# Routed experts: the third pair's rows also picked in SBUF, the first reads of scattered rows one pair later

## The reference, cut to what matters

```
h = LayerNorm(ALPHA * h + mix)                    # 520 rows of 1024
h = LayerNorm(ALPHA * h + HierMoE(h))
# HierMoE: best of 4 groups, then the top 2 of its 8 experts
hid = silu(x @ w_gate[e]) * (x @ w_up[e])         # 1024 -> 256, 32 experts
y  += weight[row, e] * (hid @ w_down[e])          # 256 -> 1024
```

## Time and profile before

| what | us |
|---|---|
| median of three runs | 1031.05 |
| lowest, highest | 1030.75, 1032.7 |
| the profiled execution: device time | 1032.45 |
| the profiled execution: its span | 1030.6 |
| mixer, up to the first weights of the experts | about 656 |
| experts, 656 to the end of the last `down` | about 328 |
| gather of results and last LayerNorm | about 46 |

### The profile page before, as it was taken

One profiled execution on the slowest core, in us unless ns is written; L12 is line 12 of the kernel. 1 busy time (PEld: TensorE's weight loads), 2 busy tenths in 40 slices (PEclk: granted clock), 3 DMA queues, 4 the chain that ended last, 5 costly groups with the idle time before them and its releaser, 6 DMA issues.

```text
span 1030.6 us, 11835 instructions
## 1 busy us (share of the span) xinstructions
PE 838.6 (81%) x4513; PEld 578.1 (56%) x4513; DVE 469.7 (46%) x1025; ACT 265.1 (26%) x654; POOL 183.6 (18%) x146
## 2 busy tenths in 40 slices
PE   6999899999967788699999899878199978856910
PEld 5987789888846666478888444555133323321300
DVE  6996476575648665674344143350021101100158
ACT  4221444343452267354321011100011100000100
POOL 2663534341045540000000000020000000000030
PEclk9999899999979888899999899969599989978965
DMA  8322264451251123551622200599889999999452
GB/s 293 98 63 72 87 241 164 164 184 62 95 182 50 30 83 131 205 206 74 245 82 82 82 0 1 202 424 423 341 334 430 424 423 428 425 377 426 167 186 83
DMA packets 38809, 207.92 MB, mean 202 GB/s; under 512 B 9069, under 2 KB 9677, under 8 KB 28193
## 3 DMA queue, kind: packets, MB, share of 16 engines
q1 hardware_dynamic: 29056, 172.28, 42.9%
q0 software_dynamic: 5136, 18.36, 5.2%
q10 hardware_dynamic: 4560, 16.52, 4.0%
HBM read 169.00 MB, written 38.05 MB: 201 GB/s over the span
## 4 chain that ended last, share of the span: by engine, by line
PE 39%; issue 31%; DVE 19%; DMA 4%; POOL 2%; ACT 2%; SPq 1%; POOLq 0%; DVEq 0%; ACTq 0%
PE bank L561 7%; PE bank L568 7%; PE bank L570 6%; PE bank L569 6%; DVE r_f L1424 5%; DMA y_f<-scr_bc 2%; PE bank L722 2%; PE bank L754 1%; DVE y_f L1503 1%; DMA x_f<-in_conv_state 1%; PE bank L682 1%; DVE y_f L1572 1%; POOL scr_x L2085 1%; PE bank L753 1%; PE bank L758 1%
## 5 line engine op out<-in xcount | busy, mean ns | idle before, releaser
L568 PE MATMUL bank<-r_r,w_r 128*128 128x268 f32 x416 | 125.3, 301 | 10.8 <-DVE w_r L1401 10.2
L569 PE MATMUL bank<-y_r,w_r 128*128 128x268 f32 x416 | 121.6, 292 | 0.0
L570 PE MATMUL bank<-r_r,w_r 128*128 128x268 f32 x416 | 121.5, 292 | 0.0
L945 PE MATMUL bank<-x_f,r_f 128*64 128x512 f32 x256 | 87.6, 653 | 13.4 <-DMA x_f<-in_w_gu 10.8
L569 PE MATMUL bank<-w_r,r_r 128*128 128x512 f32 x240 | 96.6, 402 | 0.0
L568 PE MATMUL bank<-x_r,r_r 128*128 128x512 f32 x200 | 82.4, 412 | 16.0 <-DVE w_r L1704 12.0
L568 PEld LDWEIGHTS bank<-r_r,w_r 128*128 128x128 f32 x416 | 81.4, 196 | 15.9 <-DVE w_r L1401 10.2
L1900 DVE TENSOR_TENSOR y_f<-bank,y_f 128x256 f32<-128x256 f32 x17 | 7.2, 424 | 166.4 <-ACT y_f L1327 154.2
L569 PEld LDWEIGHTS bank<-y_r,w_r 128*128 128x128 f32 x416 | 81.3, 196 | 0.0
L570 PEld LDWEIGHTS bank<-r_r,w_r 128*128 128x128 f32 x416 | 81.1, 195 | 0.0
L570 PE MATMUL bank<-x_r,w_r 128*128 128x512 f32 x200 | 80.7, 404 | 0.0
(11 more groups left out here) (334 smaller groups left out, 1561.1 us busy)
## 6 DMA issues: line engine op xcount, KB each, us to landing
x_f<-in_w_gu SPq DMA_DIRECT2D x16, 2048.0 KB, 31.6
w_f<-in_w_gu SPq DMA_DIRECT2D x12, 2048.0 KB, 22.3
w_f<-in_w_f SPq DMA_DIRECT2D x26, 512.0 KB, 4.4
scr_x<-y_f SPq DMA_DIRECT2D x25, 512.0 KB, 6.1
w_f<-in_w_d SPq DMA_DIRECT2D x12, 1024.0 KB, 24.1
x_f<-in_w_d SPq DMA_DIRECT2D x11, 1024.0 KB, 29.5
w_f<-in_w_t SPq DMA_DIRECT2D x5, 2048.0 KB, 8.1
y_f<-in_w_gu SPq DMA_DIRECT2D x5, 2048.0 KB, 28.9
```

The source lines that it names most:

```text
L568: pe.matmul(out, ah, bh, start=start, stop=False)
L569: pe.matmul(out, ah, bl, start=False, stop=False)
L570: return pe.matmul(out, al, bh, start=False, stop=stop)
L945: ins = pe.matmul(out[half, :], XT[:, k, half], wgu[s][:, k, :], start=(k == 0), stop=(k == KC - 1))
```

## The change

`N_HOT` becomes 3, so pair 2 is picked out of `h1` as pairs 0 and 1 are. Its ten DVE instructions are not in `dve_route` but at the head of `dve_experts`, with matrices `hot_last[t]` in the place of buffer X[0]; `iota_hot` gets a third part; `near` moves to another address. ACT's wait on `sc_out` and its first two reads (now for pairs 3 and 4) come after pair 1, and the read for pair 4 is no longer issued inside pair 1. The scaling of `h1` by ALPHA on DVE (L1915, L1916) comes in pair 3 and no more in pair 2.

```diff
-N_HOT = 2
+N_HOT = 3
+N_HOT0 = 2
...
+        hot_last = [cut(R1 + P * t, P) for t in range(NT)]
+        iota_hot = cut(RX + N_HOT0 * P, N_HOT * P)
...
             def pick_x(b):
...
-                    pe.wait_ge(S["hot_dv"], t + 1)
+                    pe.wait_ge(S["hot_dv"], NT * (b // N_HOT0) + t + 1)
+                    chosen_rows = hot[t][0:r, P * b:P * (b + 1)] if b < N_HOT0 else hot_last[t][0:r, :]
...
                     act.wait_ge(S["xtr_mm"], b + 2)
-                    if b and b + 3 < FIRST or b == FIRST:
+                    if b > 1 and b + 3 < FIRST or b == FIRST:
                         load_x(act, b + 3 if b < FIRST else FIRST + 2)
...
-                if b == 0:
+                if b == 1:
                     act.wait_ge(S["sc_out"], 16 * 2 * NT)
                     load_x(act, N_HOT)
                     load_x(act, N_HOT + 1)
...
+            for t in range(NT):
+                dve_link[0](v.tensor_scalar(hot_last[t], iota_hot[:, N_HOT0 * P:], near[:, t:t + 1], None, ALU.is_equal))
+                v.scalar_tensor_tensor(hot_last[t], iota_hot[:, N_HOT0 * P:], near[:, NT + t:NT + t + 1], hot_last[t],
+                                       ALU.is_equal, ALU.add).then_inc(S["hot_dv"], 1)
             v.wait_ge(S["xtr_mm"], 1)
             v.wait_ge(S["rt_dv"], 4)
             empty_x("xt_ev")
```

More of the change, by code:

```diff
@@ L277, in build @@
         far, base = more(2 * NT), more(2 * NT)
-        near = more(2 * NT)
+        near = cut(RX + (N_HOT0 + N_HOT) * P, 2 * NT)
         thr8 = more(EPG)
@@ L290, in build @@
         wdn = [cut(b, DE // P, D) for _, b in slot_at]
-        hot = [*(cut(R1 + 2 * D + N_HOT * P * t, N_HOT * P) for t in range(NT - 1)), cut(RX, N_HOT * P)]
-        iota_hot = cut(RX + N_HOT * P, N_HOT * P)
+        hot = [*(cut(R1 + 2 * D + N_HOT0 * P * t, N_HOT0 * P) for t in range(NT - 1)), cut(RX, N_HOT0 * P)]
+        hot_last = [cut(R1 + P * t, P) for t in range(NT)]
+        iota_hot = cut(RX + N_HOT0 * P, N_HOT * P)
         X, XT = [cut(R1, D), cut(C1, D)], cut(R1 + D, KC, P)
@@ L927, in pick_x @@
                     r = tile_rows(t)
-                    pe.wait_ge(S["hot_dv"], t + 1)
+                    pe.wait_ge(S["hot_dv"], NT * (b // N_HOT0) + t + 1)
+                    chosen_rows = hot[t][0:r, P * b:P * (b + 1)] if b < N_HOT0 else hot_last[t][0:r, :]
                     for k in range(KC):
                         ins = pe.matmul(pb[k // 4][:, (k % 4) * P:(k % 4 + 1) * P], h1[0:r, t, k * P:(k + 1) * P],
-                                        hot[t][0:r, P * b:P * (b + 1)], start=(t == 0 and k % 4 == 0),
+                                        chosen_rows, start=(t == 0 and k % 4 == 0),
                                         stop=(t == NT - 1), skip_group_check=True)
@@ L1869, in dve_route @@
             for t in range(NT):
-                link(v.tensor_scalar(hot[t], iota_hot, near[:, t:t + 1], None, ALU.is_equal))
-                v.scalar_tensor_tensor(hot[t], iota_hot, near[:, NT + t:NT + t + 1], hot[t], ALU.is_equal, ALU.add)\
-                 .then_inc(S["hot_dv"], 1)
+                link(v.tensor_scalar(hot[t], iota_hot[:, 0:N_HOT0 * P], near[:, t:t + 1], None, ALU.is_equal))
+                v.scalar_tensor_tensor(hot[t], iota_hot[:, 0:N_HOT0 * P], near[:, NT + t:NT + t + 1], hot[t],
+                                       ALU.is_equal, ALU.add).then_inc(S["hot_dv"], 1)
             link(v.tensor_reduce(extra, over[:, :, :], AX, ALU.add))
```

## The result

The changed kernel takes 1019.46 us (median of four runs, 1016.01 to 1021.6) against 1031.01 for the kernel before on the same chip: ratio 0.9881, 95% interval 0.9849 to 0.9914, a gain of 11.6 us where 10.2 were forecast. Left out of all times are single executions that took hundreds of us longer than the others of their kernel (1449 us once in `hole_back`, 1691 and 4586 for the kernel before).

The account below looks back on a forecast made before the run. The prediction took the weights' stream to bound the experts' stage: closing its hole (8.5 to 9.6 us) and dropping pair 2's read (1.3) give 10.2, so 1032.45 becomes 1022.2 profiled, median 1020.8 us, range 1018.5 to 1025.5.

Parts of the forecast that it names:

- The bound: Experts' stage: the weights' stream limits it; PE's 22.4 us wait counts only through the hole it tears there.
- The 0.24 us of `iota_hot`: Routing chain: one more instruction for the third part delays pair 0 by 0.24 us, hidden by SP's full queue.
- the 6 us in hand: Pair 3's rows, expected at 744.2 us, could land as late as 750 without opening a hole in the stream.
- the first wait for weights: PE in the experts' stage: expected still around pair 8 or earlier, and longer than before.
- The hole: DMA between 740 and 755 us, share 0.44 and 151 GB/s: expected to close, worth 8.5 to 9.6 us.
- The sum: Experts' stage: closed hole plus pair 2's dropped read, together 9.7 to 10.8 us, taken as 10.2.
- the read's 1.2: Weights' stream: pair 2's read of 0.52 MB falls away, forecast as 1.3 us at 417 GB/s.
- the hole by share: DMA's dry stretch sized by engine share, 15 x (1 - 0.44 / 1.01) = 8.5 us.
- The late read: Rival: pair 3's rows land after 750 us, moving part of the hole; at 755, time 1025.8 us; chance 0.12.
- The port case: Rival: `hot_last` on DVE locks POOL's scatter issue, ending the scatter up to 4.0 us later; 1022.5 us; chance 0.05.
- The extra half block: Rival: weights issued behind it at 929.05 us do not move forward; gain 7.4 us, time 1023.6; chance 0.07.
- The prediction's one pairing: POOL's DMA issue at 690.60 us, 0.96 us long, with DVE's copy starting inside it: taken as no stretching.

Follow-up runs that it names:

- `hole_back`: Changed kernel with one more wait on SP: pair 4's down weights wait until pair 3's rows are turned; 1019.05 us, ratio 0.9891 to the kernel before.
- `hole_long`: Changed kernel with SP holding pair 4's down weights and all later loads until pair 4's rows are turned; 1034.35 us, ratio 1.005 to the kernel before.
- `less_bytes`: Changed kernel reading only the first half of the down weights of experts 14 to 17, all compute instructions kept; 1015.74 us.
- `pe_extra`: Changed kernel with the eight transposes for pair 5 made six times; 1019.25 us.
- `fourth_pick`: Changed kernel with pair 3's rows picked too, ten more DVE instructions, and the first reads of rows after pair 2; 1019.71 us.
- `before_again`: The kernel before the change, unchanged, run once more; 1028.41 us, ratio 0.9992.

## Why the prediction was right

**The bound.** Shown: a hole without the stall costs (`hole_long`); 5.0 us worth of bytes less save 4.0 to 5.8 us by the count and 3.5 by the median time (`less_bytes`); 4.4 us more of PE work cost nothing that can be told from none (`pe_extra`).

**The steps.** The 0.24 us of `iota_hot` are 0.20: three instructions now take 0.68 us against 0.48. `hot_last` takes five times 0.58 = 2.9 us, inside the 2.0 to 4.0, and DVE still waits 1.27 us before pair 0's copy:

```profile
668.41 0.68 DVE L1861 TENSOR_SCALAR x_f<-bank 128x128 f32<-128x128 f32 x3
...
680.56 0.28 DVE L1926 TENSOR_SCALAR r_f<-x_f 128x128 f32<-128x128 f32 x1
680.88 0.35 DVE L1927 SCALAR_TENSOR_TENSOR r_f<-x_f,r_f 128x128 f32<-128x128 f32 x1
681.14 0.28 DVE L1926 TENSOR_SCALAR r_f<-x_f 128x128 f32<-128x128 f32 x1
...
684.84 0.69 DVE L1900 COPY r_f<-bank 128x512 f32<-128x512 f32 x1 [1.27 <-PE bank L933]
```

The pick takes 9.2 us from its start to that of the hidden turn (713.22 to 722.45), as forecast. From pair 0's start, SP's loads for pairs 4 and 5 go out after 41.4 and 48.3 us, as forecast (41.4 and 48.3). The read of pair 3 went out 43.9 us behind pair 0's start against 42.7, took 11.2 us (729.54 to 740.73) against 10, and from the transposes to gate and up lie 8.25 us against 6.8: the granted clock had fallen to the lower level, 0.50, in the wait.

```profile
739.00:741.00 2.00, 0.27 (x2) 0.28 (x3) 0.00 (x0) 0.00 (x0) 0.00 (x0) 0.50 1.06 444
```

So pair 3 started 3.9 us later than forecast (63.4 against 59.4 from pair 0's start). This cost nothing, as the 6 us in hand said, and it is evidence of its own: from pair 0's start PE gained 6.9 us at pair 3, the stage 10.8 (339.1 to 328.3). One sign came otherwise: the first wait for weights is not at pair 8 or earlier but at pair 9 (5.29 us at 828.95), which fits: PE gained less than the stream and so caught up with it later.

**A term that may be too small.** The hole closed wholly. The sum, 10.2 (9.7 to 10.8), against 11.2 in the first pair of profiles; over both pairs the counts are 373.7 and 362.5 on average, again 11.2. By bytes the hole is 15 x (1 - 151 / 426) = 9.7 us, and the stretch behind it, 412 against 424 GB/s over 25 us, adds 0.7; with the read's 1.2 that is 11.6. By this reading I took a value too near to the hole by share and ended the hole at 755 us too early. It is not shown: the counts of one kernel differ by 1.8 us, the later runs on one chip have medians of 1029.06 and 1019.25, 9.8 us apart, and the read's 1.2 us never showed by itself (`fourth_pick`).

**The rivals.** The late read did not come: the rows landed 55.1 us behind pair 0's start, and the forecast had room until 58.4 (750). The port case did not come either: from POOL's first issue to the first read of rows pass 49.3 us in both profiles of the changed kernel and 48.7 and 49.3 in the two of the kernel before. POOL's ten issues take 12.4 us from first to last end, against 12.3 before, one at 1.05 us and the others at 0.89 to 0.98, and the slowest of the scatter's DMAs lands after 37.8 us and not 37.3:

```profile
681.49 0.98 POOL L2092 DMA_INDIRECT scr_x<-r_f,small_f  x1 [0.31 <-issue]
682.77 1.05 POOL L2092 DMA_INDIRECT scr_x<-r_f,small_f  x1 [0.30 <-issue]
```

The Trainium skill ("SBUF — State Buffer", section "SBUF: two separate sides") lets a VectorE instruction in a two-port mode hold up such issues. Here ten instructions from SBUF to SBUF beside three of them left no more than that 0.1 us, and no row shows whether they work in such a mode. The prediction's one pairing was not the only one in its trace: two short instructions from SBUF to SBUF (0.21 and 0.18 us, at 685.5) stand beside POOL's first issue there, which took 0.95 us. The extra half block moved with the stream: pair 13's wait is 7.02 us against 7.68, and from its gate and up to the end lie 86.3 us in both profiles.

## What to carry to other kernels

Where a stage is bound by a stream of loads, as this one is, a stall of the computing engine costs only the hole that it makes in the stream, by way of the loads that its late instructions release; size the gain by the DMA rows (missing bytes by the full rate) and not by the wait's length. Follow the hole until the rate is back at its full value. And to prove it, hold the loads back without touching the computing engine, and see that the hold outlasts the loads already queued.

## What was not expected

The start of the experts' stage, the same program but for one DVE instruction, differs between profiles by 7.7 us (685.63 to 693.36), and the times of one kernel by 9 us (`before_again`, 1024.21 to 1033.33). Comparing the first two profiles, part of it arises where DVE waits for a read of `scr_bc` (11.44 us up to 415 before, 9.45 up to 413 after), and part where PE's granted clock falls or does not behind a wait of 2.1 us (0.83 in the kernel before from 570 to 590 us, 1.00 after the change at the same work). A device time alone would have put the gain of the first profile at 16.4 us; the count gives 11.2.

A hold of the weights made the reads of rows faster (7.2 us against 11.2 for pair 3's), and so undid most of itself (`hole_back`).
